# Closing a projection's chunks in turn with whole ones, and the norm's total behind two groups instead of four, in a three-mixer transformer kernel

## The reference

```python
# first block, i = 0 (fox) and 1 (mla)
h = rmsnorm(x, norm_mix[i])
p = h @ w_in
o_mix = fox_mixer(...)  if i == 0 else mla_mixer(...)     # 12 heads of 64, causal softmax
o_mem = memory_cross(p[..., -256:], k_mem, v_mem, ...)
x = x + concatenate([o_mix, o_mem], -1) @ w_out[i]
u = rmsnorm(x, norm_ffn[i]) @ ffn_w_up[i]                 # 1024 -> 5632
u = depthwise_conv3(u) + conv_b
gate, val = split(u, 2)
x = x + (silu(gate) * val) @ ffn_w_down[i]                # 2816 -> 1024
# second block
x = x + 0.5 * swiglu(rms_norm(x, g_ffn1), w_ffn1_gate, w_ffn1_up, w_ffn1_down)
q, k, v, u, mq = split(rms_norm(x, g_mix) @ w_in)
y_attn = sliding_window_attention(rope_partial(rms_norm(q)), rope_partial(rms_norm(k)), v, sinks)
y_conv = silu(layer_norm(depthwise_conv31(a * sigmoid(gate)) + b_dw))   # a, gate = split(u)
y_mem = memory_cross_attention(mq, mk, mv)
x = x + concatenate([y_attn, y_conv, y_mem], -1) @ w_out
x = x + 0.5 * swiglu(rms_norm(x, g_ffn2), w_ffn2_gate, w_ffn2_up, w_ffn2_down)
```

## Time and profile before

| | us |
|---|---|
| median of 3 runs (2227.41 to 2228.83) | 2228.28 |
| the profiled execution's own time | 2224.88 |
| its span | 2223.1 |
| TensorE busy | 2117.9 (95%) |
| VectorE busy | 1274.8 (57%) |
| ScalarE busy | 952.9 (43%) |
| GpSimd busy | 33.7 (2%) |
| mean granted TensorE clock | 0.982 |
| bytes read from HBM | 183.25 MB, 83 GB/s |

### The profile page before, as it was taken

The page is one execution under the profiler, slowest core; times in us unless marked ns, Lnnn a source line. Parts: engine busy times, 40 slices in busy tenths (PEclk is TensorE's granted clock), DMA queues, the critical chain, the costliest instruction groups (busy, mean ns, idle before and its releaser), DMA issues.

```text
span 2223.1 us, 30649 instructions
## 1 busy us (share of the span) xinstructions
PE 2117.9 (95%) x11378; PEld 1759.9 (79%) x11378; DVE 1274.8 (57%) x2212; ACT 952.9 (43%) x1912; POOL 33.7 (2%) x71
## 2 busy tenths in 40 slices
PE   6999998999999798989999999999998889999999
PEld 6888786888889676768888888888888667888887
DVE  6645567746764775567367544434447865543442
ACT  6645544423445764444244343223344564332331
POOL 0000001000000010000000000000001000000000
PEclk9999999999999899989999999999999999999999
DMA  6212132332333010222333233333232112333332
GB/s 203 73 53 58 49 91 62 102 103 90 95 100 105 15 39 29 71 76 95 100 94 100 95 95 100 95 97 98 90 100 62 39 30 81 105 99 91 103 96 91
DMA packets 101670, 187.36 MB, mean 84 GB/s; under 512 B 11408, under 2 KB 12048, under 8 KB 101264
## 3 DMA queue, kind: packets, MB, share of 16 engines
q1 hardware_dynamic: 101520, 185.39, 27.5%
HBM read 183.25 MB, written 2.10 MB: 83 GB/s over the span
## 4 chain that ended last, share of the span: by engine, by line
PE 47%; DVE 3%; ACT 2%; issue 1%; POOL 0%; DVEq 0%; ACTq 0%; POOLq 0%
PE PSA L1541 15%; PE PSA L1542 14%; PE PSA L1543 14%; PE PSA L1559 1%; PE PSA L1560 1%; PE PSA L1561 1%; DVE RS L1694 1%; DVE WL L1705 0%; ACT PP L2043 0%; ACT WH L1974 0%; PE PSA L1648 0%; PE PSA L1663 0%; DVE CV L1694 0%; PE PSA L1630 0%; DVE XT L1846 0%
## 5 line engine op out<-in xcount | busy, mean ns | idle before, releaser
L1705 DVE TENSOR_TENSOR WL<-RAW,WH 128x512 fp32r<-128x512 f32 x681 | 459.2, 690 | 470.7 <-ACT WH L1974 447.1
L1974 ACT ACTIVATE WH<-RAW 128x512 fp32r<-128x512 f32 x681 | 414.7, 626 | 485.5 <-PE PSA L1543 407.1
L1541 PE MATMUL PSA<-HNh,WH 128*128 128x512 f32 x1440 | 566.3, 393 | 28.5 <-DVE CV L1694 21.2
L1542 PE MATMUL PSA<-HNl,WH 128*128 128x512 f32 x1440 | 562.9, 391 | 0.0
L1543 PE MATMUL PSA<-HNh,WL 128*128 128x512 f32 x1440 | 562.8, 391 | 0.0
L1541 PEld LDWEIGHTS PSA<-HNh,WH 128*128 128x128 f32 x1440 | 272.0, 189 | 89.6 <-DVE CV L1694 22.0
L1542 PEld LDWEIGHTS PSA<-HNl,WH 128*128 128x128 f32 x1440 | 272.0, 189 | 57.3 <-issue 1.2
L1543 PEld LDWEIGHTS PSA<-HNh,WL 128*128 128x128 f32 x1440 | 271.8, 189 | 56.9
L1541 PE MATMUL PSA<-Gh,WH 128*128 128x512 f32 x704 | 274.3, 390 | 0.9 <-DVE Gl L1869 0.9
L1542 PE MATMUL PSA<-Gl,WH 128*128 128x512 f32 x704 | 273.9, 389 | 0.0
L1543 PE MATMUL PSA<-Gh,WL 128*128 128x512 f32 x704 | 273.9, 389 | 0.0
(11 more groups left out here) (253 smaller groups left out, 2478.1 us busy)
## 6 DMA issues: line engine op xcount, KB each, us to landing
RAW<-in_w SPq DMA_DIRECT2D x681, 256.0 KB, 2.6
XT<-in_x SPq DMA_DIRECT2D x8, 256.0 KB, 5.3
MT<-in_mem SPq DMA_DIRECT2D x2, 1024.0 KB, 6.4
out_x<-XT SPq DMA_DIRECT2D x8, 256.0 KB, 2.1
PAR<-in_par SPq DMA_DIRECT2D x1, 207.0 KB, 7.2
CB<-in_cb SPq DMA_DIRECT2D x1, 100.0 KB, 7.1
PAR<-in_par SPq DMA_DIRECT2D x1, 84.5 KB, 2.0
CONST<-in_const SPq DMA_DIRECT2D x1, 65.0 KB, 5.3
```

The source lines that it names most:

```text
L1541: pe.matmul(out, wh, xh, start=(a["start"] and c == 0), stop=False)
L1542: pe.matmul(out, wh, xl, start=False, stop=False)
L1705: dve.tensor_tensor(l[:, :], r[:, :], h[:, :], ALU.subtract).then_inc(done.sem("split.dve"), 1)
L1974: act.activation(h[:, :], r[:, :], ACT.Copy).then_inc(done.sem("split.act"), 1)
```

## The change

1. `out_parts`: the four chunks opened early are 0, 2, 4, 6 instead of 0, 1, 2, 3, and each is closed just ahead of a whole odd chunk: 0, 1, 2, ... 7.
2. In `projection`, the square of a chunk and its addition are put 5 and 6.2 tiles behind its closing, instead of all eight behind the last chunk's parts. The additions follow the order in which they were planned, and the total waits for the last of them.
3. `ffn` has no `ahead` any more: the first pair alone stands before the total in every FFN (before: two pairs in FFN0, FFN1 and FFN3, one in FFN2), and for all later pairs scale and conversion of the gate group are written right behind its matmuls, ahead of the up group.
4. In mixer 3 the K turn's lag goes from 4 to 7 and the Q turns' from 2 to 4.5; the sink step comes right behind the fourth maximum; and for jobs with two heads on a tile (`both`) the broadcast of the reciprocals stands behind `values` and the turn.

The description of the change also says that V is left to ScalarE in the second mixer. No line of the diff does that, and the steps of mixers 1 and 2 are the same before and after.

```diff
 def out_parts(first, late):
-    return ([(c, first, late) for c in range(OPEN)] + [(c, late, 8) for c in range(OPEN)]
-            + [(c, first, 8) for c in range(OPEN, 8)])
+    return ([(2 * c, first, late) for c in range(OPEN)]
+            + [x for c in range(OPEN) for x in ((2 * c, late, 8), (2 * c + 1, first, 8))])
...
             def total(self):
                 if not self.summed:
                     self.summed = True
-                    need([self.fed(KC - 1)])
+                    need(self.all_fed())
...
                     for xs in ((slice(0, 2),) if t.joint else (slice(0, 1), slice(1, 2))):
                         step("pmax", key + (xs.start,), job=job, i=i, xs=xs, S=S, tile=key, before=tokens, src=t.scores(xs))
+                    if i == 3 and job.sink is not None:
+                        step("psink", jkey, job=job, S=S, last=key + (0 if t.joint else 1,))
...
+            def older(self, scored, turned):
+
+                ends = turned and turned[1] == 3
+                late = ends and self.jobs[turned[0]].both
+                cost = self.sums(*turned) if ends and not late else 0
+                cost += self.values(*turned) if turned else 0
+                cost += self.turn(*scored) if scored else 0
+                return cost + (self.sums(*turned) if late else 0)
...
             def fed(d, c):
                 added(name, layer, c, first, d)
-                norm.got.append(("project.dve", (name, layer, c, first)))
+                norm.got[c] = ("project.dve", (name, layer, c, first))
                 norm.part(c, norm.free, 1.3)
+                after(5, lambda: norm.square(c))
+                after(6.2, lambda: norm.add(c))
...
             until([("part.dve", (norm.name, KC - 1))], 0)
-            for c in range(KC):
-                after(0.5 + 1.3 * c, lambda c=c: norm.square(c))
-                after(1.7 + 1.3 * c, lambda c=c: norm.add(c))
...
-                    if (s, q) == (0, 0):
-                        opened = [both(n) for n in range(ahead)]
-                    groups = opened[q] if q < len(opened) else both(q)
-                    for x, (g, b) in enumerate(groups):
+                    def up_group(x):
+                        return dense(cols[x][0], layer, cols[x][1], last.out, freed[x])
+                    first = (s, q) == (0, 0)
+                    opened = [up_group(x) for x in range(2)] if first else []
+                    for x in range(2):
+                        g, b = opened[x] if first else up_group(x)
                         last.scaled(g, b)
...
-                      [([yt[:, t, :] for t in range(4)], BK[0][:, :], BK[1][:, :], par("gk2"), lambda: [])])
+                      [([yt[:, t, :] for t in range(4)], BK[0][:, :], BK[1][:, :], par("gk2"), lambda: [])], lags=(2, 2, 3.5, 7, 2.5))
...
-                 for x in range(2)], h, QR[:, 3 + p, :], 2.0)
+                 for x in range(2)], h, QR[:, 3 + p, :], 4.5)
```

More of the change, by code:

```diff
@@ L618, in part @@
                 step("part", (self.name, c), norm=self, c=c, got=self.got[c], free=free, h=h)
-                self.out.append((h, l, [("part.dve", (self.name, c))]))
+                self.out[c] = (h, l, [("part.dve", (self.name, c))])
                 def low():
@@ L636, in add, with all_fed @@
             def add(self, c):
-                step("feed", (self.name, c), norm=self, c=c, sq=("feed", self.name, c))
+                step("feed", (self.name, c), norm=self, c=c, sq=("feed", self.name, c), last=self.adds[-1:])
+                self.adds.append(c)
+            def all_fed(self):
+                return [self.fed(c) for c in range(KC)]
             def feed(self, c, got):
-                self.got.append(got)
+                self.got[c] = got
                 if self.free is not None:
@@ L646, in finish @@
             def finish(self, free):
-                if not self.out:
+                if None in self.out:
                     for c in range(KC):
@@ L791, in values, with sums, spread @@
                     psum.take(("pvals", jkey), [("pmix.mul", ckey)], 6)
[L792 to L801, removed]
-                step("pvals", key, job=job, i=i, jkey=jkey, t=t)
-                return 0.3 * job.tiles[i][1] / 128 + (0.8 if i == 3 else 0)
+                step("pvals", key, job=job, i=i, jkey=jkey, t=t)
+                return 0.3 * job.tiles[i][1] / 128
+            def sums(self, n, i):
+                jkey, ckey = (self.id, n), (self.id, self.jobs[n].chunk)
+                need([("precip.dve", jkey)])
+                aux = aux_bank(("pbcast", jkey), [("pspread.act", ckey)])
+                step("pbcast", jkey, S=PSTAT[pstats.of[jkey]], bank=aux)
+                def spread():
+                    x = tmp.take(("pmix", ckey), [("pmix.dve", ckey)])
+                    step("pspread", ckey, jkey=jkey, bank=aux, F=TMP[x], before=tmp.before["pmix", ckey])
+                    after(0.4, lambda: self.mix(n))
+                after(0.3, spread)
+                return 0.8
             def recip(self, n):
@@ L825, in run @@
                         if scored or turned:
-                            yield (self.values(*turned) if turned else 0) + (self.turn(*scored) if scored else 0)
+                            yield self.older(scored, turned)
                             scored, turned = None, scored
@@ L830, in run @@
                     cost = self.score(*tile) if tile else 0
-                    cost += self.values(*turned) if turned else 0
-                    cost += self.turn(*scored) if scored else 0
+                    cost += self.older(scored, turned)
                     scored, turned = tile, scored
@@ L876, in projection, with ffn @@
             until([("part.dve", (norm.name, KC - 1))], 0)
-            for c in range(KC):
-                after(0.5 + 1.3 * c, lambda c=c: norm.square(c))
-                after(1.7 + 1.3 * c, lambda c=c: norm.add(c))
-        def ffn(f, gate, up, down, layer, off, last, conv, weight, norm, between=None, ahead=1):
+        def ffn(f, gate, up, down, layer, off, last, conv, weight, norm, between=None):
             ring[:], aux_ring[:] = [0, 1, 2, 3, 4], [5, 6]
@@ L884, in ffn @@
             for s in range(2):
[L885 to L890, removed]
-                    return [dense(n, layer, col, last.out, t)
-                            for (n, col), t in zip(((gate, 128 * c), (up, off + 128 * c)), freed)]
+                parts = []
                 for q in range(HALF):
@@ L1223, in program @@
         last, norm = norm, Norm("mix1", XT, "mix1")
-        ffn(0, "ffn_w_up", "ffn_w_up", "ffn_w_down", 0, FF, last, True, 1.0, norm, angles, 2)
+        ffn(0, "ffn_w_up", "ffn_w_up", "ffn_w_down", 0, FF, last, True, 1.0, norm, angles)
         step("tables", 0)
@@ L1382, in program @@
         last, norm = norm, Norm("f1", XT, "f1")
-        ffn(1, "ffn_w_up", "ffn_w_up", "ffn_w_down", 1, FF, last, True, 1.0, norm, ahead=2)
+        ffn(1, "ffn_w_up", "ffn_w_up", "ffn_w_down", 1, FF, last, True, 1.0, norm)
         step("tables", 1)
@@ L1718, in vector @@
                     w.wait_ge(*done("square.act", key))
[L1719 removed]
+                    if not a["last"]:
                         dve.tensor_copy(nm.acc, S[:, 0:nm.N]).then_inc(done.sem("feed.dve"), 1)
                     else:
[L1722 removed]
+                        w.wait_ge(*done(*nm.fed(a["last"][0])))
                         dve.tensor_tensor(nm.acc, nm.acc, S[:, 0:nm.N], ALU.add).then_inc(done.sem("feed.dve"), 1)
```

18 lines of the change are left out of this document (8 added, 10 removed).

## The result

The changed kernel takes 2213.38 us (median of four runs, 2210.43 to 2215.57), beside 2228.56 for the kernel before. The ratio is 0.9935, with a 95% interval of 0.9919 to 0.995: 0.65% faster, about 15 us. The forecast was 2213.7 us. The profiled execution has a span of 2208.6 us against 2223.1.

The account below looks back on a forecast made before the run. TensorE bounds the kernel (busy 2117.9 of 2223.1 us), so only its waits and the slow clock behind them count. Terms -1.4 - 8.5 - 0.5 + 5.8 - 10.0 = -14.6 took 2228.3 to 2213.7 us; range 2201 to 2226.

Parts of the forecast that it names:

- The starts: FFN0's last low part comes 5.9 us later, FFN1's 4.0; TensorE waits about 3.3 us ahead of chunks 5 and 7.
- The clock: Slow clock behind the new waits for low parts: 2.2 us charged to each start; FFN1's start already pays it.
- Rival B: Starts are cheap: each costs 2 us instead of 5.9, with no clock charge; 2203 us, chance 0.15.
- rival E: The next group's bank still waits for the last conversions, so FFN0's and FFN1's gains are lost; 2224 to 2228 us, chance 0.05.
- FFN0: First conv FFN: total at 330.7 instead of 333.64, bank wait of 10.59 us gone; -1.4 us, bounds +3 to -4.
- FFN1: Second conv FFN: total at 932.7 instead of 939.48, its eleventh `Gl` sooner; -8.5 us, bounds -3 to -11.
- The wait at the first `down`: In FFN0 and FFN1, a quarter us goes, and its like in the second halves; -0.5 us over four halves.
- FFN3: Two new waits of about 3.3 us and 2.2 of clock replace waits of 0.99 and 2.07; +5.8 us, bounds 0 and +10.
- Mixer 3: Two Q-turn waits for `YC` and the third broadcast's 3.63 us go or shrink, with clock; -10.0 us, bounds -3 and -16.
- less than 5 us here: Sign of a wrong prediction: the stretch from 1701 to 1856, in mixer 3's stage, shrinks by less than 5 us.
- The rival with -3 for the mixer: Mixer 3 gains 3 us instead of 10, or starts cost 2 us more each; 2220 to 2227 us, chance 0.18.
- The rule on eight banks: Use all eight PSUM banks: fewer groups ahead of the total should cost, losing FFN1's gain; sum 2222 us.

Follow-up runs that it names:

- e4: The changed kernel with mixer 3 wholly as before (old lags, sink and broadcast places); 2219.95 us, ratio 0.9975 to the kernel before.
- e2: The changed kernel with the old `ffn`, four groups ahead of the total in FFN0, FFN1 and FFN3; 2234.48 us, ratio 1.004 to the kernel before.
- e1: The kernel before with only the new `ffn`; `projection`, `out_parts` and mixer 3 as before; 2208.2 us, ratio 0.9923.
- e6: The changed kernel with only the first three chunks' sums early and four groups ahead of FFN3's total; 2203.61 us, ratio 0.9894 to the kernel before.
- e12: The changed kernel with all sums behind the last part and four groups ahead of FFN3's total; 2197.64 us, ratio 0.9871 to the kernel before.
- e9: The changed kernel with each chunk's square and addition on GpSimd right behind its closing; 2218.0 us, ratio 0.9963 to the kernel before.
- e3: The changed kernel with all squares and additions behind the last part, as before; 2201.28 us, ratio 0.989 to the kernel before.

## Why the prediction was right, and where not

The time was right to 0.3 us, and that closeness is luck: mixer 3 was forecast 4.6 us too good, and the FFNs and the end of mixer 1 together about as much too bad. The direction and the mechanism of the two conv FFNs, which carry most of the gain, were right.

- **The starts.** The chain through both queues was right: 24.4 us from the first closing to the last low part, 24.7 forecast, 18.8 before. The waits were 2.9 and 2.2 us instead of 3.3 each. The clock was charged once per start; it fell behind the first wait of FFN0 and not behind the second, and in FFN3 behind the second and not the first. Rival B (cheap starts) falls by these rows, rival E by the missing waits for `CV`.
- **FFN0**, -1.4 forecast, -3.35 measured. The total came at 327.70 instead of 330.7: 0.65 from mixer 1, 0.3 from the low part, and 2 us because after the second wait the tiles ran at full clock. The sum had taken 2.2 us of clock between the last low part and the total, where it had already been paid ahead of it. From the total to the first `down` the step was right, 120.1 us for 120.2. The first `down` itself so came 4.5 us sooner than before; the stage wins less since a new wait of 0.83 us for `XT` stands at its end, ahead of mixer 2, which nothing in the forecast had.
- **FFN1**, -8.5 forecast, -10.2 measured. Counted from its own start the total was forecast at 928.7 and came at 928.14, and total to first `down` was 117.1 against 117.7. The rest is in the second half, which won 0.5 us where 0.25 was forecast. The wait at the first `down`, which was to go, did not: 0.25 and 0.23 us became 1.45 in FFN0 and 0.35 in FFN1.
- **FFN3**, +5.8 forecast, +5.1 measured.
- **Mixer 3**, -10.0 forecast, -5.4 measured: the step that failed. I took the waits for `YC` as gone, with the clock behind them. They were the first link of a chain from rotated Q over turn and split to the scores, and moving the turn back moved the wait to `BQL`, 2.55 and 1.07 us. Only the bank wait at the broadcast went whole. Of TensorE's idle time 6.1 us went, where the three waits alone were put at 8.4. How far the term was off is less sure than that step: -5.4 by this stage, -7.8 beside e4, and e4's whole time would allow the forecast's 10. The prediction named less than 5 us here as a sign that it is wrong; 5.4 is too near to that, by what this stage varies, to be called a pass. The rival with -3 for the mixer had this in words, "a wait removed from a chain often turns up at the next link", at 0.18.
- **The rule on eight banks** of the Trainium skill (Perfetto Trace Analysis, Matmul Optimizations), by which the sum would have been 2222, did not come true here: with four groups ahead (e2) the bank waits of 7.6 and 10.6 us are back, and with two (e1) the conv FFNs are 6.6 and 11.5 us faster. But fewer open groups were right only where VectorE's chain behind the total decides the end: in FFN3 four groups are as good (e6) or better (e12).
- **What the prediction did not ask.** It priced the early sums as a cost of the change and never set the total's own wait for late sums against it. That comparison was in reach: the additions before ended 8.7 us behind the last low part, two groups take 6.1, so late sums cost 2.6 us of wait, against 5.9 forecast for early ones.

Open: why the slow clock follows the waits in FFN0 and not in FFN3 with three early sums, what couples the lags and the broadcast in mixer 3, and what the order of conversions earns beside the number of groups. The early sink was not tried alone.

## What to carry to other kernels

Work that is drawn forward to be out of the way later should go behind, not into, a chain that feeds the bound engine: idle time in an in-order queue is not free time if the idle stretch is a link of that chain. Make the bound engine's inputs first, then do the bookkeeping while it works on them; a wait of 2.3 us at the total was cheaper than 5.4 us more ahead of the last part. And when a wait on one link goes, look at the next link before you count it as won.

## What the runs showed of the hardware

GpSimd beside VectorE was the surprise: an engine that was 2% busy, given two operations per chunk, made VectorE's splits, which read two tensors of SBUF, 1.66 and 1.77 us long instead of 0.68 (e9), and undid the gain of e3. And the clock does not follow from the length of a wait alone. Stretches of the changed kernel (us, busy by engine, granted clock, DMA share, GB/s), the first behind a wait of 2.90 us, the second behind 2.20, the third behind 2.91, the fourth behind 2.90:

```profile
316.40:319.40 3.00, 2.84 (x6) 1.59 (x6) 2.32 (x4) 0.76 (x3) 0.00 (x0) 0.50 0.06 12
321.40:324.40 3.00, 2.96 (x13) 2.46 (x14) 2.90 (x5) 1.32 (x3) 0.00 (x0) 1.00 0.42 126
1843.00:1846.00 3.00, 1.92 (x6) 0.97 (x6) 2.60 (x5) 0.76 (x2) 0.00 (x0) 1.00 0.00 0
1849.00:1852.00 3.00, 3.00 (x9) 2.35 (x8) 2.37 (x4) 0.63 (x1) 0.00 (x0) 0.50 0.59 170
```

Waits of nearly the same length, 2.90 and 2.91 us, were followed by 0.50 (1.2 GHz) at one place and 1.00 (2.4 GHz) at the other. In these runs a forecast could charge the clock per start only on average. In mixer 3 the same program took 196.3 us at a mean granted clock of 0.97 and 200.3 at 0.95.
